# 56 transposes of the identity between the token transposes and the first expert's products

## The reference

```
h  = RMSNorm(x) * (1 + scale1) + shift1
x += gate1 * ( sig(g_a) * DiffAttention(h) + sig(g_b) * ChunkGMLP(h) ) @ w_out
h2 = RMSNorm(x) * (1 + scale2) + shift2
x += gate2 * ExpertChoiceMoE(h2)
```

```
xe  = h2[idx]                                        # 80 x 1024, the chosen tokens
hid = silu(xe @ w_gate[e]) * (xe @ w_up[e])          # 80 x 2048
ye  = (hid @ w_down[e]) * gates                      # 80 x 1024
out[idx] += ye
```

## Time and profile before

| | |
|---|---|
| three runs | 1854.56, 1858.3, 1857.57 us |
| median | 1857.57 us |
| profiled execution: its time | 1857.18 us |
| profiled execution: its span | 1855.3 us |
| TensorE busy (PE) | 1768.0 us, 95% of the span |
| weight loads on TensorE (PEld) | 1248.0 us, 67%, beside the matmuls |
| VectorE busy (DVE) | 1417.2 us, 76% |
| ScalarE busy (ACT) | 1119.4 us, 60% |
| GpSimd busy (POOL) | 384.0 us, 21% |
| mean granted clock of TensorE | 0.976 |

### The profile page before, as it was taken

One profiled execution on the slowest core, in us unless ns is written; L12 is line 12 of the kernel. 1 busy time (PEld: TensorE's weight loads), 2 busy tenths in 40 slices (PEclk: granted clock), 3 DMA queues, 4 the chain that ended last, 5 costly groups with the idle time before them and its releaser, 6 DMA issues.

```text
span 1855.3 us, 24101 instructions
## 1 busy us (share of the span) xinstructions
PE 1768.0 (95%) x8645; PEld 1248.0 (67%) x8645; DVE 1417.2 (76%) x1372; ACT 1119.4 (60%) x1179; POOL 384.0 (21%) x202
## 2 busy tenths in 40 slices
PE   5799999999999895899999999999999999999996
PEld 2677787778888785566666666666666666666664
DVE  1588626357666565799899899899899899989994
ACT  2443222257666523677777777777777777777773
POOL 1255403000000000030330231131132132033021
PEclk9899999999999896899999999999999999999998
DMA  9345643322212334899999999999999999999993
GB/s 330 102 136 197 226 168 125 95 90 83 90 40 71 114 114 168 300 369 382 379 376 386 380 379 385 374 379 382 382 376 384 381 374 384 381 379 381 383 376 109
DMA packets 264945, 506.14 MB, mean 273 GB/s; under 512 B 10364, under 2 KB 30036, under 8 KB 264888
## 3 DMA queue, kind: packets, MB, share of 16 engines
q1 hardware_dynamic: 256328, 483.39, 72.0%
q0 software_dynamic: 8560, 21.98, 4.5%
HBM read 485.92 MB, written 19.42 MB: 272 GB/s over the span
## 4 chain that ended last, share of the span: by engine, by line
PE 90%; DVE 3%; ACT 2%; DMA 2%; issue 1%; SPq 1%; POOL 0%; DVEq 0%; ACTq 0%; POOLq 0%
PE banks L1583 27%; PE banks L1584 26%; PE banks L1585 26%; PE banks L1765 2%; PE banks L1752 2%; PE banks L1675 2%; DMA raw<-in_w_ada 1%; PE banks L1602 1%; PE banks L1913 1%; PE banks L1900 1%; PE banks L1714 0%; DVE var L1064 0%; DMA xg<-xn_scr,idx_g 0%; PE banks L1616 0%; PE banks L1861 0%
## 5 line engine op out<-in xcount | busy, mean ns | idle before, releaser
L1441 DVE TENSOR_TENSOR w_lo<-raw_x,w_hi 128x2048 fp32r<-128x2048 f32 x192 | 437.5, 2286 | 65.8 <-ACT w_hi L966 64.0
L1441 DVE TENSOR_TENSOR w_lo<-raw,w_hi 128x2048 fp32r<-128x2048 f32 x189 | 430.9, 2287 | 35.4 <-ACT w_hi L966 31.7
L966 ACT ACTIVATE w_hi<-raw 128x2048 fp32r<-128x2048 f32 x189 | 363.0, 1920 | 110.8 <-PE banks L1585 107.5
L966 ACT ACTIVATE w_hi<-raw_x 128x2048 fp32r<-128x2048 f32 x192 | 368.1, 1917 | 86.1 <-PE banks L1585 84.7
L1583 PE MATMUL banks<-w_hi,xe_hi 128*80 128x512 f32 x1024 | 406.3, 397 | 2.2 <-issue 2.2
L1584 PE MATMUL banks<-w_hi,xe_lo 128*80 128x512 f32 x1024 | 404.1, 395 | 0.0
L1585 PE MATMUL banks<-w_lo,xe_hi 128*80 128x512 f32 x1024 | 400.3, 391 | 0.0
L1559 POOL DMA_INDIRECT out<-yeg,idx_l x32 | 146.4, 4576 | 832.2 <-DVE yeg L1403 832.2
L1583 PE MATMUL banks<-w_hi,h_hi 128*128 128x512 f32 x560 | 226.1, 404 | 6.1 <-DVE kT_lo L1091 3.1
L1584 PE MATMUL banks<-w_hi,h_lo 128*128 128x512 f32 x560 | 219.7, 392 | 0.0
L1585 PE MATMUL banks<-w_lo,h_hi 128*128 128x512 f32 x560 | 219.5, 392 | 0.0
(11 more groups left out here) (236 smaller groups left out, 2055.7 us busy)
## 6 DMA issues: line engine op xcount, KB each, us to landing
raw<-in_w_gate_e SPq DMA_DIRECT2D x80, 1024.0 KB, 7.6
raw_x<-in_w_down_e SPq DMA_DIRECT2D x80, 1024.0 KB, 7.7
raw<-in_w_up_e SPq DMA_DIRECT2D x64, 1024.0 KB, 7.8
raw_x<-in_w_up_e SPq DMA_DIRECT2D x64, 1024.0 KB, 8.0
raw_x<-in_w_gate_e SPq DMA_DIRECT2D x48, 1024.0 KB, 6.4
raw<-in_w_down_e SPq DMA_DIRECT2D x48, 1024.0 KB, 8.0
raw<-in_w_in SPq DMA_DIRECT2D x28, 1024.0 KB, 5.5
raw<-in_w_ada SPq DMA_DIRECT2D x24, 1024.0 KB, 7.4
```

The source lines that it names most:

```text
L966: nc.scalar.activation(w_hi[:, j % NSPLIT], raw_slot(slot), ACT.Copy).then_inc(hi_done, 1)
L1441: nc.vector.tensor_tensor(w_lo[:, j % NSPLIT], raw_slot(EXPERT_SLOT[j % NRAWE]), w_hi[:, j % NSPLIT], ALU.subtract).then_inc(lo_done, 1)
```

## The change

A constant `WARMING` is added, and on TensorE's stream a loop of 56 transposes. They come after both token transposes of expert 0 and after the wait for the last bank of the list, and before the first instruction of `expert(0)`. Each has the identity as its input and as its other operand, and writes the first 128 columns of bank 0. Nothing reads them. They wait for nothing and signal nothing.

```
--- before.py
+++ after.py
@@ -232,6 +232,7 @@
+WARMING = 56
 STEPS = [("M", 0), ("B", 0), ("C", 0), ("C", 1), ("T", 0), ("M", 1), ("T", 1), ("Q", 0), ("M", 2), ("W", 0, 0), ("T", 2), ("M", 3), ("W", 1, 0), ("T", 3), ("M", 4),
...
@@ -1904,6 +1905,8 @@
                 token_transposes(0, half)
             wait_emptied(pe, P2[-1])
 
+            for _ in range(WARMING):
+                nc.tensor.transpose(bank(0)[:, 0:P], ident[:, :], ident[:, :])
 
             def hid_transposes(e, fb):
                 pe.wait_ge(hid_ready, e * 4 + (fb + 1))
```

## The result

The changed kernel takes 1860.06 us (median of 22 runs, 1857.89 to 1861.83), the kernel before 1856.02 us (22 runs, 1852.75 to 1858.3). The ratio of the changed kernel's time to the other's is 1.0020, 95% interval 1.0014 to 1.0027: 3.7 us slower, between 2.6 and 5.0. The forecast was slower, with 1861.0 us and a range from 1857.0 to 1867.0.

The account below looks back on a forecast made before the run. TensorE was taken to bound the kernel. A first product 6.1 us late, less 2.7 us from warm products, gave 1860.6 us; with 2.2 back the median would be 1861.5. Forecast 1861.0 us, range 1857.0 to 1867.0.

Parts of the forecast that it names:

- What bounds the kernel: Expert stage, 750.00 to 1839.90 us: TensorE sets the pace, so each microsecond it starts later delays the end equally.
- The place: Seam before expert 0: queue order puts the 56 behind the gather, with only 2.3 us of idle time to fill.
- The price of the block: 56 transposes at 0.215 us cold and 0.109 warm: 8.4 us, 4.7 of it cold and 3.7 warm.
- The rise: TensorE's clock going from 0.50 to 1.00 within the block, forecast 4.7 us after the block's start at about 747.65.
- the ends of 3.5 and 5.8: Shortest and longest time taken for the clock to rise after 747.65, in us, from rises in the earlier trace.
- The late start and what comes back: First expert products start 6.1 us later but warm, which gives back 2.7 us against the profiled execution.
- The sum for the profiled pair: Late start less warm products, 6.1 - 2.7 = +3.4 us, against the profiled execution's 1857.18 us.
- The middle value for the medians: With a middle gain of 2.2 us for other executions' cold starts: 6.1 - 2.2 = +3.9 us on the median.
- The two edits costed at nothing: Repeated writes to the same 128 columns of bank 0, and fetching 112 more instructions: both taken as zero.
- Transposes that leave the clock alone: Rival, 12%: the block stays cold at 12.0 us, products start 9.7 us late and cold, 1866.9 us.
- The swallowed delay: Rival, 8%: transfers pace the expert stage, so TensorE's later start loses nothing, about 1857.2 us.
- The block inside the gather's wait: Rival, 3%: the 56 run before the gather lands and the clock stays up, 2.7 us gained, 1854.5 us.

## Why the prediction was right

**What bounds the kernel.** Right. A late first product went to the end in full: 5.8 us in the changed kernel's pair, 5.8 more with the block doubled. The stage absorbs nothing, though its DMA share reads 1.03.

**The place.** Right, and it is what decided the sign. The queue's order puts the 56 behind the gather, and the same 56 moved ahead of the wait for it cost nothing that the timed runs show.

**The price of the block.** 8.4 us forecast, 8.2 measured. The per-transpose prices of other tiles (0.215 and 0.109) held for the identity and for 56 writes to the same columns: 56 in 8.45 us leaves no room for a stall between them.

**The rise.** 4.7 us after the block's start was forecast, 4.4 measured. With ten transposes it came 4.2 us after their start (746.9 to 751.1), in the moved block 5.3 us after its start (737.25 to 742.5), with the block doubled 3.6, all between the ends of 3.5 and 5.8. The middle was a choice between rows; that this profile fell near it was luck, within a spread of 1.7 us between the runs.

**The late start and what comes back.** 6.1 forecast, 5.8 measured; 2.7 forecast, 2.7 measured. The sum for the profiled pair was +3.4 and came out as +3.1. The middle value for the medians was +3.9, and 3.7 was measured. This doesn't show that the kernel before is often less cold than in its profile, as I had assumed: 3.1 lies within the interval of the 3.7 (2.6 to 5.0), and there is one profile of that kernel.

**Absolute numbers.** The forecast of 1861.0 stood on a median of three runs, 1857.57; over 22 runs it is 1856.02, 1.5 lower, so the forecast lies 0.9 above the measured 1860.06 although the difference was right. Two signs in the changed profile were given as positions, a first product near 756 and a last one 3 to 4 us after 1839.9. They came at 754.16 and 1841.41, the last only 1.5 later, because the stages ahead of the seam were 1.6 us faster in that execution. They hold only when counted from the token transposes.

**The two edits costed at nothing** cost nothing: no new wait showed. ScalarE's wait for the first chunk moved along, and the conversions were ready in time.

**The rivals.** Transposes that leave the clock alone: refuted, since the rise at 750.3 lies inside a block of transposes only. By the Trainium skill, "TensorE: Matmul & The Clock Gate", Part 4 on PE-mode transposes, it should not have come; here the measurement decides against it, for 128x128 float32 transposes. The swallowed delay: refuted by the 112 transposes. The block inside the gather's wait: not what the code does. My price for that case, 1854.5 or 2.7 us gained, didn't come out either: the moved block measured 1856.40, no change. A step that failed in it was the guess, from one row of 3.1 idle microseconds at 1.00, that the clock would outlast the seam; it fell at 749.4, and a gain clear of the noise came only with transposes in the seam as well.

The sign was a narrow call. The effect lies right at the 0.2% from which I counted it as slower.

## What to carry to other kernels

Ask of warming work where it stands in its engine's queue, not what it is meant to overlap: here 56 transposes behind a wait cost 5.8 us to win 2.7, and the same work ahead of the wait cost nothing. Size it by the idle time that it may fill and by the time to the rise, and look in the trace at whether the clock is still up when the real work begins; here it took 14 transposes in the seam to keep it up. The most that can be won on the products is the cold ones times the difference of the two paces, 14 x 0.19 us here, and 0.6 us more on the token transposes where the clock is up before them. Where the added work lies on the path for longer than what it wins, the kernel is slower.

## What the runs showed of the hardware

- TensorE can be busy without a gap and stay at the lower clock: through 23.7 us of weight loads and 2-column matmuls it stayed at 0.50, while under 128-column transposes at the same pace of 0.21 us it rose after 3.6 to 5.3 us. The profile's PE share reads full in both.
- A plain float32 matmul with 2 columns shows as two passes, 0.212 us each at 0.50 (23.77 us for 112), while a float32 transpose is one.
- With the moved block the clock fell at 749.4 us with the products 0.5 us away, after a seam that held eight small transposes, a pause of 0.8 us between their groups and one of 1.6 us behind them; with 14 more transposes in the seam it stayed up.
